# Weight products by three 256-column matmuls in place of one of 512 and one of 256

## The chip, the cores and the metric

The kernel runs on one core of a Trainium2 chip. The metric is the device time of one execution in microseconds, as the median of several runs.

## What is computed

A two-layer decoder trunk with a batch of 1, 256 tokens, and a width of 2048, all in float32. Each layer has a token-mixing half and an MLP half, both with an RMS norm ahead and behind. Cut to what matters:

```python
h = rms_norm(x, norm_mix_pre[i])
z = h @ w_comb                                # 2048 x 6400: 16 RWKV-7 heads and 8 attention heads
y_r, v_r = rwkv7_mix(token_shift(z[..., :N_SHIFT], shift_mu[i]), ...)
y_a = moba_attention(q, k, v)                 # of z[..., N_SHIFT:N_IN]
y = jnp.concatenate([y_r, y_a], axis=-1) @ w_out[i]
x = x + rms_norm(y, norm_mix_post[i])
h = rms_norm(x, norm_mlp_pre[i])
m = jnp.square(jax.nn.relu(h @ w_up[i])) @ w_down[i]     # 2048 -> 8192 -> 2048
x = x + rms_norm(m, norm_mlp_post[i])
```

## The kernel before

Activations lie transposed: 128 features on the partitions, 256 tokens along a row. A product with a weight matrix is made of **weight tiles** of 128 x 128. To keep precision with the fast format fp32r, weights and activations are each split in two parts, high and low. A product is high x high, plus high weights x low activations, plus low weights x high activations.

**Weights.** SyncE fetches 128 x 1024 values at a time, eight weight tiles, into one of four slots `raw[r]` (function `fetch`). ScalarE (ACT) rounds the slot to its high part `whi[r]` (`hi`, L886), and VectorE (DVE) subtracts to get the low part `wlo[r]` (`lo`, L1131). In the mixer GpSimd (POOL) takes two of every twelve low parts (L442). The split runs three slots ahead of TensorE (PE). A slot is free again when `slot_used` counts it.

**Activations.** `hT` and `mT` hold for each 128 features the high and the low part side by side, 2 x 256 columns. So one 512-column matmul with the high weight gives high x high in columns 0 to 255 of a PSUM bank, and high x low in columns 256 to 511. A second matmul of 256 columns adds low weights x high activations to columns 0 to 255. Both are in `tick`, L537 and L538, and for the last of 16 steps the order is turned round, L538 and L540. The profile shows one LDWEIGHTS (PEld) for each MATMUL, 16347 of either.

```python
if not last:
    mm(bank[b0 + b][:, :], whi[r][:, cols], pair, start=first, stop=False)
m = mm(bank[b0 + b][:, 0:SEQ], wlo[r][:, cols], act[:, kt, 0, :], start=False, stop=False)
if last:
    m = mm(bank[b0 + b][:, :], whi[r][:, cols], pair, start=False, stop=True)
```

**Groups.** A `group` is 16 such steps over the input features for two output tiles of 128 features, in two PSUM banks. Four banks let two groups alternate. When a group ends, its result is taken out in two steps: ACT copies the right halves of the two banks to `xl` (`halves`, L894), which counts `half_out`, and DVE adds the left halves (`sums`, L1137), which counts `tile_out`. PE waits for `tile_out` before it writes a bank again.

**Stages of a layer.** First the small projections of 256 (layer 1 also 32) columns ("lora"); then the pairs; then the output projection; then the MLP in four quarters, each of eight up groups and eight down groups. In the up groups DVE adds the halves (L1496), squares the positive part (L1499), ACT writes the high part (L1094) and DVE the low part (L1503). In the down groups DVE adds the halves (L1514), and then adds the sum to `yo` (L1519). Between the stages the norms run: squares on ACT (L920), column sums on PE (L583, L586), and the scaling on DVE.

**Pairs.** The eight pairs of a layer (two RWKV heads of 64 and one attention head of 128 each) go through `mixer`, a long chain of small steps over PE, ACT, DVE and POOL. PE fills the gaps of the chain with steps of three groups of the input projection (`fill`, `pair_ticks`): 7 steps after the first small matmuls (L622 to L624), then it waits for `t1` of DVE (L633), 4 more, then it waits for `btl` (L643), and so on. The order of each engine is written out by hand. `finish(-1)`, at the head of the mixer on ACT and DVE, takes out the group that ended last; `finish(0)` and `finish(1)` take out the other two further down. On DVE, `finish(-1)` stands ahead of the clamp of the key norm (L1202), its reciprocal (L1204), the decay (L1207), the scan (L1209) and `t1` (L1218). On ACT it stands ahead of the tanh of the decay (L952), which DVE's L1207 waits for.

## Time and profile before

| | |
|---|---|
| median of 3 runs | 2931.75 us (2930.35 to 2931.97) |
| span of the profiled execution, first to last instruction | 2927.5 us |
| PE busy, matmuls | 2826.8 us (97%), 16347 instructions |
| PE busy, weight loads | 2377.9 us (81%), 16347 instructions |
| DVE busy | 1805.9 us (62%) |
| ACT busy | 1282.0 us (44%) |
| POOL busy | 327.2 us (11%) |
| TensorE clock | mean 0.989 of full speed |

No time of the profiled execution is given apart from its span, which is 4.2 us below the median; that remainder lies outside the first and the last instruction. Busy time of PE runs from an instruction's start to its modelled end, and matmuls overlap: the distance from one start to the next tells what a matmul costs in a stream, and it is shorter than the mean duration shown. In a timeline a row with x2 is two instructions in a row of one group, shown with the start of the first and their common duration. A wait is shown as the idle time before an instruction and the one that released it.

### The profile page before, as it was taken

The page shows a single profiled execution, that of the slowest core. Times are in us where ns is not written, and L with a number is a line of the kernel's source. Part 1 is how long each engine was busy: PE and PEld are TensorE (multiplying, and loading weights), DVE is VectorE, ACT ScalarE, POOL GpSimd, SP SyncE. Part 2 cuts the span into 40 slices and gives each one's busy share as a digit, 9 for nine tenths or more (in the row PEclk, how much of TensorE's full clock was granted, in tenths as well). Part 3 has the DMA queues.
Part 4 walks back from the last instruction along what each step waited for, and adds up shares of the span by engine and source line. Part 5 has one row for each costly group of instructions (what it writes and reads, how often), then busy time and mean ns, then how long its engine had stood idle before and what let it go on. Part 6 is the DMA issues. An engine that isn't in the chain of part 4 may idle for free.

```text
span 2927.5 us, 50952 instructions
## 1 busy us (share of the span) xinstructions
PE 2826.8 (97%) x16347; PEld 2377.9 (81%) x16347; DVE 1805.9 (62%) x3008; ACT 1282.0 (44%) x2144; POOL 327.2 (11%) x448
## 2 busy tenths in 40 slices
PE   7999999998999999999989999999989999999997
PEld 6777778886888888888767788887868888888886
DVE  6666666656655656556676666666576556565655
ACT  5434333444544444444453343344444444444443
POOL 3111111102000000000132222221020000000002
PEclk9999999999999999999999999999999999999998
DMA  6333333333656555555533333332436565555653
GB/s 183 97 88 92 101 92 88 96 121 110 193 186 186 184 187 180 192 181 186 155 108 98 88 90 93 93 90 87 139 113 192 184 187 183 187 184 187 186 182 112
DMA packets 518313, 415.91 MB, mean 142 GB/s; under 512 B 19422, under 2 KB 515696, under 8 KB 518256
## 3 DMA queue, kind: packets, MB, share of 16 engines
q1 hardware_dynamic: 515888, 412.88, 45.5%
q0 software_dynamic: 2368, 2.32, 0.3%
q8 instruction: 30, 0.49, 0.1%
q14 instruction: 27, 0.22, 0.0%
HBM read 413.03 MB, written 2.10 MB: 142 GB/s over the span
## 4 chain that ended last, share of the span: by engine, by line
PE 89%; DVE 8%; issue 1%; ACT 1%; POOL 0%; DMA 0%; DVEq 0%; ACTq 0%; POOLq 0%; SPq 0%
PE gemm_bank L537 45%; PE gemm_bank L538 24%; PE gemm_bank L540 3%; PE mix_bank L697 2%; PE mix_bank L686 2%; PE mix_bank L695 2%; PE mix_bank L658 1%; DVE b_yo L1172 1%; DVE b_rn L1204 1%; PE mix_bank L659 1%; PE mix_bank L715 1%; PE mix_bank L719 1%; DVE b_yo L1155 1%; PE mix_bank L729 1%; PE mix_bank L725 1%
## 5 line engine op out<-in xcount | busy, mean ns | idle before, releaser
L537 PE MATMUL gemm_bank<-b_hT,b_whi 128*128 128x512 f32 x3420 | 1273.2, 411 | 28.1 <-DVE b_hT L1152 14.4
L1131 DVE TENSOR_TENSOR b_wlo<-b_raw,b_whi 128x1024 fp32r<-128x1024 f32 x745 | 908.0, 1232 | 498.0 <-ACT b_whi L886 496.7
L886 ACT ACTIVATE b_whi<-b_raw 128x1024 fp32r<-128x1024 f32 x777 | 806.3, 1055 | 489.4 <-PE gemm_bank L538 484.1
L538 PE MATMUL gemm_bank<-b_hT,b_wlo 128*128 128x256 f32 x3648 | 1016.8, 283 | 0.0
L537 PE MATMUL gemm_bank<-b_mT,b_whi 128*128 128x512 f32 x2400 | 856.7, 400 | 1.7 <-DVE b_yo L1137 1.7
L537 PEld LDWEIGHTS gemm_bank<-b_hT,b_whi 128*128 128x128 f32 x3420 | 647.0, 189 | 201.4 <-issue 51.7
L538 PE MATMUL gemm_bank<-b_mT,b_wlo 128*128 128x256 f32 x2560 | 706.8, 281 | 0.0
L538 PEld LDWEIGHTS gemm_bank<-b_hT,b_wlo 128*128 128x128 f32 x3648 | 693.7, 190 | 14.2 <-issue 5.3
L537 PEld LDWEIGHTS gemm_bank<-b_mT,b_whi 128*128 128x128 f32 x2400 | 451.0, 188 | 110.6 <-issue 4.3
L538 PEld LDWEIGHTS gemm_bank<-b_mT,b_wlo 128*128 128x128 f32 x2560 | 483.8, 189 | 7.1
L894 ACT ACTIVATE b_xl<-gemm_bank 128x256 f32<-128x256 f32 x389 | 127.8, 381 | 302.2 <-PE gemm_bank L540 296.8
L478 POOL TENSOR_TENSOR b_gs<-b_gs,b_zt 128x256 f32<-128x256 f32 x56 | 38.1, 681 | 1498.4 <-ACT b_zt L920 1495.2
L996 ACT ACTIVATE b_U<-mix_bank 64x128 f32<-64x128 f32 x64 | 17.3, 271 | 239.9 <-PE mix_bank L715 239.9
L978 ACT ACTIVATE b_yo<-mix_bank 128x128 f32<-128x128 f32 x160 | 44.6, 279 | 165.9 <-PE mix_bank L686 165.9
L697 PE MATMUL mix_bank<-b_yo 128*128 128x64 f32 x640 | 115.0, 273 | 0.0
L1275 DVE COPY_PREDICATED b_yo<-b_lvl,mix_bank 128x128 f32<-128x128 uint8 x128 | 42.6, 333 | 104.3 <-PE mix_bank L697 104.3
L442 POOL TENSOR_TENSOR b_wlo<-b_raw,b_whi 128x1024 fp32r<-128x1024 f32 x32 | 76.1, 2378 | 188.7 <-DVE b_wlo L1131 172.4
L695 PE MATMUL mix_bank<-b_yo 128*128 128x64 f32 x512 | 95.3, 267 | 0.0
L697 PEld LDWEIGHTS mix_bank<-b_yo 128*128 128x128 f32 x640 | 93.4, 192 | 0.7
L435 POOL TENSOR_TENSOR b_yo<-b_zt 128x256 f32<-128x256 f32 x32 | 20.9, 670 | 645.0 <-DVE b_zt L1137 645.0
L1514 DVE TENSOR_TENSOR b_xl<-gemm_bank,b_xl 128x256 f32<-128x256 f32 x128 | 48.4, 420 | 71.6 <-ACT b_xl L894 71.6
L1496 DVE TENSOR_TENSOR b_AR<-gemm_bank,b_xl 128x256 f32<-128x256 f32 x128 | 48.5, 421 | 65.2 <-ACT b_xl L894 65.2
(229 smaller groups left out, 2627.8 us busy)
## 6 DMA issues: line engine op xcount, KB each, us to landing
b_raw<-in_w_up SPq DMA_DIRECT2D x256, 512.0 KB
b_raw<-in_w_down SPq DMA_DIRECT2D x256, 512.0 KB
b_raw<-in_w_in SPq DMA_DIRECT2D x384, 256.0 KB
b_raw<-in_w_out SPq DMA_DIRECT2D x48, 512.0 KB
b_raw<-in_w_out SPq DMA_DIRECT2D x32, 256.0 KB
b_raw<-in_w_in SPq DMA_DIRECT2D x8, 512.0 KB
b_yo<-in_x SPq DMA_DIRECT2D x2, 1024.0 KB, 6.9
out<-b_raw SPq DMA_DIRECT2D x8, 256.0 KB, 2.5
```

Of the source, the lines that this page charges most:

```text
L442: nc.gpsimd.tensor_tensor(wlo[at][:, :], raw[at][:, :, :].rearrange("p a b -> p (a b)"), whi[at][:, :].bitcast(F32), ALU.subtract).then_in ...
L537: mm(bank[b0 + b][:, :], whi[r][:, cols], pair, start=first, stop=False)
L538: m = mm(bank[b0 + b][:, 0:SEQ], wlo[r][:, cols], act[:, kt, 0, :], start=False, stop=False)
L540: m = mm(bank[b0 + b][:, :], whi[r][:, cols], pair, start=False, stop=True)
L686: m = mm(packed(mb[2 + w][:, at:at + HEAD], lv), G[:, unit, 2, :], blocks(TT[:, unit, 0, :], lv, 0), start=True, stop=True)
L695: mm(packed(mb[w][:, at:at + HEAD], lv), TT[:, unit, 1, :], blocks(X[:, unit, :], lv, 0), start=True, stop=True)
L697: m = mm(packed(mb[w][:, P + at:P + at + HEAD], lv), X[:, unit, :], blocks(TT[:, unit, 1, :], lv, 1), start=True, stop=True)
L886: f(whi[r][:, :], raw[r][:, :, :].rearrange("p a b -> p (a b)"), ACT.Copy).then_inc(hi_done, 1)
L894: f(xl[:, b, :], bank[b0 + b][:, SEQ:2 * SEQ], ACT.Copy).then_inc(half_out, 1)
L1131: tt(wlo[r][:, :], flat(raw[r][:, :, :]), whi[r][:, :].bitcast(F32), ALU.subtract).then_inc(lo_done, 1)
L1496: tt(hid(b), bank[2 * g + b][:, 0:SEQ], xl[:, b, :], ALU.add).then_inc(up_sum, 1)
L1514: tt(xl[:, b, :], bank[2 * g + b][:, 0:SEQ], xl[:, b, :], ALU.add).then_inc(down_sum, 1)
```

## The change

In `tick` the high weight is used by two matmuls of 256 columns, with the high and with the low activations, and the low weight by one, and all three add into columns 0 to 255 of the bank. The order is the same for all 16 steps. The bank then holds the finished sum, and the halves need no adding. The same is done for the 32-column projection of layer 1.

- ACT copies each finished tile from PSUM straight to its place in `zt` or `yo` (`tiles_to`) and counts `tile_out`; `sums` is gone from DVE. As ACT now writes the places that DVE wrote, it waits ahead of it for their last readers (`free`).
- Up groups: ACT takes relu from PSUM to `AR`, then its square as the high part, while DVE squares into `xl` and subtracts.
- Down groups: ACT does nothing for the bank; DVE waits for the slot and adds the bank to `yo` at once.
- ACT's wait for `used_y` in `y_squares` is made a separate one (`wait_alone`).

```diff
@@ tick, PE
-                pair = act[:, kt, :, :].rearrange("p a b -> p (a b)")
                 for b in range(2):
                     cols = slice(256 * j + P * b, 256 * j + P * b + P)
-                    if not last:
-                        mm(bank[b0 + b][:, :], whi[r][:, cols], pair, start=first, stop=False)
-                    m = mm(bank[b0 + b][:, 0:SEQ], wlo[r][:, cols], act[:, kt, 0, :], start=False, stop=False)
-                    if last:
-                        m = mm(bank[b0 + b][:, :], whi[r][:, cols], pair, start=False, stop=True)
+                    into = bank[b0 + b][:, 0:SEQ]
+                    mm(into, whi[r][:, cols], act[:, kt, 0, :], start=first, stop=False)
+                    mm(into, whi[r][:, cols], act[:, kt, 1, :], start=False, stop=False)
+                    m = mm(into, wlo[r][:, cols], act[:, kt, 0, :], start=False, stop=last)
@@ ACT
-            def halves(k, d, tiles, b0, n=2):
+            def tiles_to(dest, k, d, b0, n=2):
                 act.wait_ge(slot_used, k + 4 * d + 1)
-                if not (isinstance(tiles, int) and tiles <= 0):
-                    act.wait_ge(tile_out, tiles)
                 for b in range(n):
-                    f(xl[:, b, :], bank[b0 + b][:, SEQ:2 * SEQ], ACT.Copy).then_inc(half_out, 1)
+                    f(dest(b), bank[b0 + b][:, 0:SEQ], ACT.Copy).then_inc(tile_out, 1)
...
+                def free(g, n):
+                    if g == -1:
+                        act.wait_ge(l_shift, 2 + 3 * l)
+                        act.wait_ge(e["pair_done"], n + 1)
+                    if g == 1:
+                        act.wait_ge(e["shifted"], 3 * n + 2)
...
                     def finish(g):
-                        halves(k + 11 + 4 * g, i * 3, t + 4 + 2 * g + i * 6, (2, 2, 0)[g + 1])
+                        free(g, PAIRS * l + i)
+                        tiles_to(place((1, 2, 0)[g + 1]), k + 11 + 4 * g, i * 3, (2, 2, 0)[g + 1])
...
+                                    f(AR[:, b, :, :].rearrange("p a b -> p (a b)"), bank[2 * g + b][:, 0:SEQ],
+                                      ACT.Relu).then_inc(up_relu, 1)
...
-                                      ACT.Copy).then_inc(up_hi, 1)
+                                      ACT.Square).then_inc(up_hi, 1)
@@ DVE
-            def sums(tiles, b0, dest, n=2):
-                for b in range(n):
-                    dve.wait_ge(half_out, tiles + b + 1)
-                    tt(dest(b), bank[b0 + b][:, 0:SEQ], xl[:, b, :], ALU.add).then_inc(tile_out, 1)
...
-                                    dve.wait_ge(half_out, T + b + 1)
-                                    tt(hid(b), bank[2 * g + b][:, 0:SEQ], xl[:, b, :], ALU.add).then_inc(up_sum, 1)
+                                    dve.wait_ge(up_relu, M + b + 1)
+                                    tt(xl[:, b, :], hid(b), hid(b), ALU.mult).then_inc(up_square, 1)
...
+                                dve.wait_ge(slot_used, k + 36 + 4 * g + qq * 64 + i * 8)
                                 for b in range(2):
-                                    dve.wait_ge(half_out, T + b + 1)
-                                    tt(xl[:, b, :], bank[2 * g + b][:, 0:SEQ], xl[:, b, :],
-                                       ALU.add).then_inc(down_sum, 1)
-                                for b in range(2):
-                                    dve.wait_ge(down_sum, M + b + 1)
                                     at = bass.ds(i * 4 + 2 * g + b, 1)
-                                    tt(yo[:, at, :], yo[:, at, :], xl[:, b, :].unsqueeze(1),
+                                    tt(yo[:, at, :], bank[2 * g + b][:, 0:SEQ].unsqueeze(1), yo[:, at, :],
                                        ALU.add).then_inc(tile_out, 1)
```

**Where instructions move, PE, end of a pair's mixer and start of the next one.** Before (L537 and L540 are the 512-column matmuls, L538 the one of 256; L622 to L624 are the first matmuls of the mixer):

```order
L537 MATMUL gemm_bank<-b_hT,b_whi 128x512
L538 MATMUL gemm_bank<-b_hT,b_wlo 128x256 x2
L540 MATMUL gemm_bank<-b_hT,b_whi 128x512
L538 MATMUL gemm_bank<-b_hT,b_wlo 128x256
L540 MATMUL gemm_bank<-b_hT,b_whi 128x512
L274 REGISTER_ALU
L274 COMPARE_AND_BRANCH
L622 MATMUL mix_bank<-b_lact,b_lw 128x256 [waits l_shift,l_tanh,m_lw_in,l_ready,m_n2_root,m_pair_done]
L623 MATMUL mix_bank<-b_lact,b_lw 128x256
L624 MATMUL mix_bank<-b_lact,b_lw 128x256
L537 MATMUL gemm_bank<-b_hT,b_whi 128x512 [waits lo_done,hi_done,tile_out]
```

With the change (L535 and L536 take the high weight, L537 the low one):

```order
L535 MATMUL gemm_bank<-b_hT,b_whi 128x256
L536 MATMUL gemm_bank<-b_hT,b_whi 128x256
L537 MATMUL gemm_bank<-b_hT,b_wlo 128x256
L535 MATMUL gemm_bank<-b_hT,b_whi 128x256
L536 MATMUL gemm_bank<-b_hT,b_whi 128x256
L537 MATMUL gemm_bank<-b_hT,b_wlo 128x256
L273 REGISTER_ALU
L273 COMPARE_AND_BRANCH
L619 MATMUL mix_bank<-b_lact,b_lw 128x256 [waits l_shift,l_tanh,m_lw_in,l_ready,m_n2_root,m_pair_done]
L620 MATMUL mix_bank<-b_lact,b_lw 128x256
L621 MATMUL mix_bank<-b_lact,b_lw 128x256
L535 MATMUL gemm_bank<-b_hT,b_whi 128x256 [waits lo_done,hi_done,tile_out]
```

Each weight tile has three matmuls instead of two; nothing else on PE changes place, and the first product after L621 still waits for `tile_out`.

**DVE at the same place.** Before:

```order
L1379 TENSOR_TENSOR b_mT<-b_yf,b_mT 128x256
L1130 REGISTER_ALU
L1131 TENSOR_TENSOR b_wlo<-b_raw,b_whi 128x1024 [waits hi_done]
L274 REGISTER_ALU
L274 COMPARE_AND_BRANCH
L1137 TENSOR_TENSOR b_zt<-gemm_bank,b_xl 128x256 [waits half_out] x2
L1202 TENSOR_SCALAR b_rn<-b_rn 128x256 [waits m_n2_root]
L1204 RECIPROCAL b_rn<-b_rn 128x256 [waits m_n2_max]
L1207 TENSOR_SCALAR b_ldc<-b_eN 128x4x64 [waits m_w_tanh]
```

With the change:

```order
L1384 TENSOR_TENSOR b_mT<-b_yf,b_mT 128x256
L1145 REGISTER_ALU
L1146 TENSOR_TENSOR b_wlo<-b_raw,b_whi 128x1024 [waits hi_done]
L273 REGISTER_ALU
L273 COMPARE_AND_BRANCH
L1209 TENSOR_SCALAR b_rn<-b_rn 128x256 [waits m_n2_root]
L1211 RECIPROCAL b_rn<-b_rn 128x256 [waits m_n2_max]
L1214 TENSOR_SCALAR b_ldc<-b_eN 128x4x64 [waits m_w_tanh]
```

The two adds, which wait for ACT's copies, are gone from between the last subtraction and the clamp.

## Rows read from the trace of the kernel before

**Rows 1.** The page, parts 1 and 4: busy time by engine; the chain that ended last

```profile
PE 2826.8 (97%) x16347; PEld 2377.9 (81%) x16347; DVE 1805.9 (62%) x3008; ACT 1282.0 (44%) x2144; POOL 327.2 (11%) x448
...
PE 89%; DVE 8%; issue 1%; ACT 1%; POOL 0%; DMA 0%; DVEq 0%; ACTq 0%; POOLq 0%; SPq 0%
...
PE gemm_bank L537 45%; PE gemm_bank L538 24%; PE gemm_bank L540 3%; PE mix_bank L697 2%; PE mix_bank L686 2%; PE mix_bank L695 2%; PE mix_bank L658 1%; DVE b_yo L1172 1%; DVE b_rn L1204 1%; PE mix_bank L659 1%; PE mix_bank L715 1%; PE mix_bank L719 1%; DVE b_yo L1155 1%; PE mix_bank L729 1%; PE mix_bank L725 1%
```

**Rows 2.** Groups of instructions, shapes apart: low matmul of every weight tile; a load

```profile
L538 PE MATMUL gemm_bank<-b_hT,b_wlo 128*128 128x256 f32 x3648 | 1016.8, 283 | 0.0
...
L538 PE MATMUL gemm_bank<-b_mT,b_wlo 128*128 128x256 f32 x2560 | 706.8, 281 | 0.0
...
L697 PEld LDWEIGHTS mix_bank<-b_yo 128*128 128x128 f32 x640 | 93.4, 192 | 0.7
```

**Rows 3.** Busy time by stretch, in the MLP: window, length, PE, PEld, DVE, ACT, POOL, clock, DMA

```profile
2400.00:2700.00 300.00, 300.00 (x1701) 260.64 (x1701) 176.59 (x240) 136.42 (x186) 0.00 (x0) 1.00 0.59 188
```

**Rows 4.** Timeline of PE, one group's end in the MLP: start us, us, instruction

```profile
1209.68 0.28 PE L538 MATMUL gemm_bank<-b_mT,b_wlo 128*128 128x256 f32 x1
1209.80 0.40 PE L537 MATMUL gemm_bank<-b_mT,b_whi 128*128 128x512 f32 x1
1210.04 0.40 PE L538 MATMUL gemm_bank<-b_mT,b_wlo 128*128 128x256 f32 x2
1210.28 0.40 PE L540 MATMUL gemm_bank<-b_mT,b_whi 128*128 128x512 f32 x1
1210.51 0.28 PE L538 MATMUL gemm_bank<-b_mT,b_wlo 128*128 128x256 f32 x1
1210.63 0.39 PE L540 MATMUL gemm_bank<-b_mT,b_whi 128*128 128x512 f32 x1
1210.86 0.39 PE L537 MATMUL gemm_bank<-b_mT,b_whi 128*128 128x512 f32 x1
1211.09 0.28 PE L538 MATMUL gemm_bank<-b_mT,b_wlo 128*128 128x256 f32 x1
1211.20 0.40 PE L537 MATMUL gemm_bank<-b_mT,b_whi 128*128 128x512 f32 x1
```

**Rows 5.** Timeline of PEld in the mixer: short matmuls with full weight tiles

```profile
319.95 0.86 PEld L697 LDWEIGHTS mix_bank<-b_yo 128*128 128x128 f32 x7
```

**Rows 6.** Timeline of ACT and DVE, start of the fourth pair's mixer, layer 0

```profile
277.94 0.66 ACT L894 ACTIVATE b_xl<-gemm_bank 128x256 f32<-128x256 f32 x2 [1.49 <-PE gemm_bank L540]
...
278.36 0.76 DVE L1137 TENSOR_TENSOR b_zt<-gemm_bank,b_xl 128x256 f32<-128x256 f32 x2 [1.15 <-ACT b_xl L894]
...
278.62 1.28 ACT L952 ACT_TABLE_LOAD   x1
...
279.03 0.78 DVE L1202 TENSOR_SCALAR b_rn<-b_rn 128x256 f32<-128x256 f32 x1
...
279.84 1.75 DVE L1204 RECIPROCAL b_rn<-b_rn 128x256 f32<-128x256 f32 x1
...
279.91 0.47 ACT L952 ACTIVATE b_eN<-mix_bank,b_drv 128x256 f32<-128x256 f32 x1
...
281.51 0.83 DVE L1207 TENSOR_SCALAR b_ldc<-b_eN 128x256 f32<-128x256 f32 x1
...
284.55 1.32 DVE L1218 SCALAR_TENSOR_TENSOR b_t<-b_sh,b_prm,b_kf 128x256 f32<-128x256 f32 x1 [0.15 <-DVE b_kf L1216]
```

**Rows 7.** Waits of PE, longest in total first: us in total, times, longest us

```profile
PE mix_bank L633 <- DVE b_t L1218: 9.9, 9, 1.5
...
PE mix_bank L643 <- DVE b_btl L1245: 7.8, 9, 1.4
```

**Rows 8.** Timeline of ACT and DVE, end of the last down projection

```profile
2901.59 0.66 ACT L894 ACTIVATE b_xl<-gemm_bank 128x256 f32<-128x256 f32 x2 [7.75 <-PE gemm_bank L540]
...
2902.01 0.76 DVE L1514 TENSOR_TENSOR b_xl<-gemm_bank,b_xl 128x256 f32<-128x256 f32 x2 [6.85 <-ACT b_xl L894]
...
2902.68 0.75 DVE L1519 TENSOR_TENSOR b_yo<-b_yo,b_xl 128x256 f32<-128x256 f32 x2
```

More of the change, by code:

```diff
@@ L793, in _ @@
                         cols = slice(VRES * kt, VRES * kt + P)
[L794 to L799 removed]
+                        into = bank[2][:, 0:SEQ]
+                        mm(into, whi[r][:, cols], hT[:, kt, 0, :], start=kt == 0, stop=False)
+                        mm(into, whi[r][:, cols], hT[:, kt, 1, :], start=False, stop=False)
+                        m = mm(into, wlo[r][:, cols], hT[:, kt, 0, :], start=False, stop=kt == KT - 1)
                     m.then_inc(slot_used, 1)
@@ L1039, in _ @@
                 k, t = start[l, "lora"]
-                group(k, 0, t, 2 * (1 - l))
+                splits(k, 0)
+                tiles_to(lambda b: zt[:, 3 + b, 1:], k + 3, 0, 2 * (1 - l))
                 if l:
@@ L1043, in _ @@
                     hi(k + LEAD)
[L1044 removed]
+                    tiles_to(lambda b: zt[:, 5, 1:], k, 0, 2, 1)
                 act.wait_ge(l_shift, 1 + 2 * l)
@@ L1064, in finish @@
                     if g < 1:
-                        halves(k + 95 + 4 * g, 0, t + 46 + 2 * g, 2)
+                        free(g, PAIRS * l + PAIRS - 1)
+                        tiles_to(place(g + 2), k + 95 + 4 * g, 0, 2)
                 mixer(l, PAIRS - 1, PAIRS * l + PAIRS - 1, t + 46,
@@ L1076, in turn @@
                     for g in range(2):
-                        group(k + 8 + 4 * g, i * 2, t + 4 + 2 * g + i * 4, 2 * g)
+                        splits(k + 8 + 4 * g, i * 2)
+                        tiles_to(hidden(i * 4 + 4 + 2 * g), k + 11 + 4 * g, i * 2, 2 * g)
                         y_squares(2 * l, 4 + 2 * g, i, t + 6 + 2 * g + i * 4)
@@ L1191, in key_norms, with mixer @@
                     ALU.mult).then_inc(e["kk_sq"], 1)
-            def mixer(l, i, n, tiles, step, finish, more=True):
+            def mixer(l, i, n, tiles, step, more=True):
                 V = n + 1
@@ L1468, in step @@
                         lo(k + 92 + j + LEAD)
-                mixer(l, PAIRS - 1, PAIRS * l + PAIRS - 1, t + 46, step, finish, False)
+                mixer(l, PAIRS - 1, PAIRS * l + PAIRS - 1, t + 46, step, False)
                 k, t = start[l, "out"]
-                hidden = lambda a: lambda b: yo[:, bass.ds(a + b, 1), :].rearrange("p a b -> p (a b)")
                 for g in range(2):
                     lo(k + 6 + g + LEAD)
-                    sums(t + 2 * g, 2 * g, lambda b: yo[:, 2 * g + b, :])
                 def turn(i):
```

60 lines of the change are left out of this document (20 added, 40 removed).

## The prediction

> **What bounds the kernel now.** First the page. PE is busy 97% of the span, and the chain that ended last runs 89% over PE; the two lines of `tick` alone make 72% of it [rows 1]. So the kernel lasts as long as PE's stream of weight products, and everything else counts only where PE stands still. Then how much of this work there is: the low matmul occurs once per weight tile, 3648 + 2560 = 6208 times [rows 2]. In a stretch of 300 us inside the MLP PE has no gap, at full clock, with 1701 matmuls, which is 850.5 weight tiles, so one tile lasts 300 / 850.5 = 0.3527 us [rows 3]; 6208 of them make 2190 us, three quarters of the span. ACT and DVE are busy for under 60% of that stretch, so their work is covered there.
>
> The timeline shows how a tile's time divides [rows 4]. From start to start a 512-column matmul takes 0.24, 0.23, 0.23 and 0.23 us (mean 0.232), and a 256-column one 0.12 or 0.11 (five of them in 0.59 us, mean 0.118). The starts are printed to 0.01 us, so these means are good to 2 or 3 ns. Half of 0.232 is 0.116: a column costs about the same in either, and there is hardly a price per matmul. The weight load of the next matmul is hidden: with a 256-column matmul over it, the next one starts 0.12 us later, and the row with x2 is two such matmuls in a row, 1210.04 to 1210.28.
>
> **The PE stream, the first term.** The change takes away 6208 matmuls of 512 columns and adds 12416 of 256, into the same columns; it leaves 768 columns per tile, and adds 6208 weight loads. What three 256-column matmuls in a row cost is not in the trace, two in a row are. Lower bound: full 128 x 128 loads under matmuls of only 64 columns follow each other at (0.86 - 0.19) / 6 = 0.112 us (0.19 is one load's own time) [rows 2, 5], so a tile could not go under 3 x 0.112 = 0.336, which is 0.0167 below now, or -104 us over all tiles. Upper bound: the row of two in a row, 0.12 each, 3 x 0.12 = 0.36, which is +0.0073, or +45 us. By columns alone a tile stays at 0.3527. I take 0.118, the mean of the five [rows 4], as nearest to what will run: 0.354 per tile, +0.0013 x 6208 = **+8 us**.
>
> The Trainium skill, "TensorE: Matmul & The Clock Gate", section on the back-to-back issue gap, gives a matmul N / 2.4 GHz plus about 2.5 ns; by that rule one matmul more per tile would cost 2.5 ns x 6208 = 15.5 us, an estimate. Rows 4 show 2 x 0.118 - 0.232 = 4 ns with an error of as much, so they neither confirm nor refute it; the time it gives stands under the rivals.
>
> **The start of each mixer, the second term.** When a group ends, ACT copies two halves (0.66 us), and DVE adds two (0.76 us) before it clamps, takes the reciprocal (1.75) and reaches the decay at 281.51 [rows 6]. The adds could not begin before 278.36, where DVE had stood idle for 1.15 us waiting for ACT's copy. Without them the clamp can start at 278.36 - 1.15 = 277.21, and with its 0.78 and the 1.75 the reciprocal is through by 279.8. Now the decay must wait for ACT's tanh, which ends at 279.91 + 0.47 = 280.38; ACT's own path (two copies, table load 1.28, tanh) is unchanged, as it copied two tiles before too. With the 0.07 us that a step from engine to engine takes here the decay starts at 280.45, **1.06 us earlier**, and with it all that follows up to `t1` (L1218). What is late next is thus ACT's table load and tanh.
>
> PE waits for exactly these products: 9.9 us in 9 places for `t1`, and 7.8 us in 9 places for `btl`, later on the same chain [rows 7], together 17.7 us, or 1.1 us for each of the 16 pairs. PE also gets its first fill after L624 some 0.3 us sooner, since `tile_out` no longer waits for an add; that only makes it arrive earlier at the same wait, so the chain's 1.06 us is the cap: 16 x 1.06 = 17. In a few pairs the wait is shorter than that, and I take **-16 us**. The new waits of `free` on ACT (`pair_done`, `l_shift`) come while ACT is idle for 1.49 us before the copy [rows 6], and PE itself waits for `pair_done` at L622; I cost them at nothing. If that cover were gone, two waits and the copies behind them would eat up to 0.66 us of the 1.06.
>
> **The ends of stages, the third term.** After the last down group ACT copies, DVE adds two halves (0.76) and then adds them to `yo` (0.75), and the squares of the norm wait for that [rows 8]. With the change DVE's second pair of adds starts when ACT's first copy does. From 2901.59 to 2902.68 that is 1.1 us, and there are two such ends. At the ends of the two output projections ACT's copies stay and the adds go: 0.76 us less a little overlap, about 0.7 each. Together 2 x 1.1 + 2 x 0.7 = 3.6. The handovers from the pairs to the output projection (twice) and into layer 1's small projection wait for the same drain, an estimated 0.5 us each, 1.4 in all. **-5 us**.
>
> **Edits without a price.** In the MLP ACT loses the copies of the down groups, and DVE the adds; `wait_alone` in `y_squares` and the different split of relu and square stand on engines with more than 40% idle time [rows 3], and PE needs a finished bank only one group (32 tiles, 11.3 us) later. Weight fetches keep their order and their pace, which PE's use of the slots sets. That cover would fail only if PE became much faster.
>
> **Sum.** 8 - 16 - 5 = -13 us, 0.4% of the span of 2927.5. That span is 4.2 us below the median of the runs, which I keep: 2931.75 - 13 = **2919 us**.
>
> **The rivals.**
> 1. *Each 256-column matmul takes 0.12 us when it follows one of its own size.* For it: the only two in a row do [rows 4]. Against it: the 512 before and after them are not longer than elsewhere, so that the whole is still 0.35 per tile. Price +45 us against the 21 gained: 2931.75 + 45 - 21 = 2956, slower. The point from which it decides: above 0.1187 us per matmul ((0.3527 + 21 / 6208) / 3) the loss outweighs the gain. With 2.5 ns per additional matmul, as by the rule above, it is 15.5 - 21, so 2926, on the border of no change. I give rival 1 a chance of 0.20.
> 2. *The stream stays as it is but the gain in the mixer doesn't come*, because ACT, which now must have its tiles out before `tile_out` and waits for `free`, gives back what DVE saves, and the chain goes on at ACT's pace. For it: after the change the decay hangs on ACT by 0.6 us more than on DVE (280.38 against 279.8). Then 8 - 5 + 0 to 5: 2932 to 2940; with the stream by columns alone it is no change. Chance 0.10.
> 3. *PE's queue cannot feed three pairs of load and matmul per tile.* There are six instructions in 0.353 us, 0.059 each, where four had 0.088. For it: PE would be bound by issue in the whole stream. Against it: the loads of rows 5, with a matmul to each, went at 0.112 / 2 = 0.056 per instruction. What an instruction costs in a long stream no row shows; at 5% over 0.059 a tile would be 0.370, +108 us: 3018. Chance 0.04.
> 4. *The stream gets faster*, towards the bound of the loads, since no matmul waits for the second half of a 512 wide row: half way to 0.336 it would be -52 - 21, so 2859. Chance 0.04. That the high weight is loaded only once for its two matmuls is possible too, and changes nothing, since loads are hidden.
> 5. My forecast, the stream between 0.1165 (half a 512) and 0.1187 us per matmul, and most of the gain: 0.62.
>
> **How the numbers follow.** The lower end: 3 x 0.1165 = 0.3495, -20 us, with the full 21 gives 2891; I take 2893, which leaves out rival 4. The upper end is rival 1's 2956; only rival 3 lies above. A measurement of this kernel can tell some 0.2%, 6 us, from no change. Faster (under 2926): the forecast and rival 4, less a part of the forecast that lies on the border, 0.62. No change: that part and half of rival 2, 0.15. Slower: rivals 1 and 3 and what is left of 2 and 1's neighbourhood, 0.23. If the likeliest case holds, its own range is 2900 to 2930.
>
> **What the profile afterwards should show.** Three starts per weight tile 0.118 us apart, and about 2550 matmuls in a full stretch of 300 us in the MLP, against 1701; fewer than 2500 speaks for rival 1 (0.120) or 3. PE's matmul count up by 6208, loads likewise. At the mixer's start no adds ahead of the clamp, the clamp at once after DVE's last subtraction, the decay waiting for ACT's tanh; PE's waits for `t1` and `btl` down from 17.7 us to a few. After the last down group one pair of DVE adds, and the norm's squares 1.1 us earlier. The prediction would be wrong if the distance of 256-column matmuls is above 0.1187, or if a pair's mixer gets shorter by less than 0.5 us at an unchanged stream.

## The result, and the profile after

| | before | with the change |
|---|---|---|
| median | 2931.12 us (2930.35 to 2931.97, 4 runs) | 2962.05 us (2961.27 to 2962.35, 4 runs) |
| span of the profiled execution | 2927.5 us | 2960.4 us |
| ratio | | 1.0106, 95% interval 1.0091 to 1.0120 |

The change costs 1.1%, 31 us. The forecast of 2919 had the wrong sign, and the time lies above the upper end of the range, 2956.

The page of the changed kernel, parts 1 and 4, for [rows 1]:

```profile
PE 2870.0 (97%) x22571; PEld 2732.7 (92%) x22571; DVE 1686.0 (57%) x2619; ACT 1244.9 (42%) x2016; POOL 324.9 (11%) x448
...
PE 90%; DVE 7%; ACT 2%; issue 1%; DMA 0%; POOL 0%; DVEq 0%; ACTq 0%; POOLq 0%; SPq 0%
```

PE has 22571 - 16347 = 6224 matmuls more: one for each of the 6208 weight tiles, and 16 for the projection of 32 columns. DVE has less work, as was meant. PE is as busy as before by share, of a longer span: the time went into PE's own work.

Busy time by stretch in the MLP (window, length, PE, PEld, DVE, ACT, POOL, clock, DMA), for [rows 3], first 300 us, then the first 250 of them; and the timeline of PE and PEld (start us, us, instruction), for [rows 4]:

```profile
2400.00:2700.00 300.00, 300.00 (x2502) 300.00 (x2501) 158.90 (x186) 128.65 (x165) 0.00 (x0) 1.00 0.59 183
2400.00:2650.00 250.00, 250.00 (x2086) 250.00 (x2085) 133.00 (x158) 108.85 (x143) 0.00 (x0) 1.00 0.60 183
```

```profile
2500.08 0.28 PE L535 MATMUL gemm_bank<-b_mT,b_whi 128*128 128x256 f32 x1
2500.20 0.28 PE L536 MATMUL gemm_bank<-b_mT,b_whi 128*128 128x256 f32 x1
2500.32 0.28 PE L537 MATMUL gemm_bank<-b_mT,b_wlo 128*128 128x256 f32 x1
2500.45 0.28 PE L535 MATMUL gemm_bank<-b_mT,b_whi 128*128 128x256 f32 x1
...
2500.09 0.19 PEld L536 LDWEIGHTS gemm_bank<-b_mT,b_whi 128*128 128x128 f32 x1
2500.21 0.19 PEld L537 LDWEIGHTS gemm_bank<-b_mT,b_wlo 128*128 128x128 f32 x1
```

At the same full clock (1.00 in both stretches) a matmul takes 300 / 2502 = 0.1199 us from start to start, and a tile 0.3597 where it took 0.3527. The prediction had named fewer than 2500 matmuls in this stretch as the sign of rival 1; 2502 lies just over it, but 300 / 0.12 is 2500 itself, so that sign was set too tight. The distance, 0.1199, is the better one. A load takes 0.19 and the next begins 0.12 later, so PEld has no gap any more (before 260.64 us of 300). Each load starts together with the matmul ahead of its own: L536's load starts at 2500.09, as L535's matmul does (2500.08), and L536's matmul at 2500.20.

Where the 32.9 us between the spans are follows from the starts of a few instructions that both programs have. The first matmul of a mixer (L622, now L619) and the column sum behind a stage (L583, now L580), from the two timelines; those around the MLP of layer 0 as rows, before and then after:

```profile
696.46 0.59 PE L583 MATMUL mix_bank<-b_gs,b_cst 128*128 128x256 f32 x2
...
1448.16 0.59 PE L583 MATMUL mix_bank<-b_gs,b_cst 128*128 128x256 f32 x2
```

```profile
702.40 0.59 PE L580 MATMUL mix_bank<-b_gs,b_cst 128*128 128x256 f32 x2
...
1467.70 0.38 PE L580 MATMUL mix_bank<-b_gs,b_cst 128*128 128x256 f32 x1
```

| from, to | before, us | after, us | difference |
|---|---|---|---|
| start, first mixer of layer 0 | 68.63 | 71.23 | +2.6 |
| seven pairs, first to last mixer (to 557.55; 562.26) | 488.92 | 491.03 | +2.1 |
| last mixer and output projection (to 696.46; 702.40) | 138.91 | 140.14 | +1.2 |
| MLP (to 1448.16; 1467.70) | 751.70 | 765.30 | +13.6 |
| to the first mixer of layer 1 (1519.31; 1538.10) | 71.15 | 70.40 | -0.8 |
| seven pairs (to 2009.78; 2029.36) | 490.47 | 491.26 | +0.8 |
| last mixer and output projection (to 2149.72; 2170.41) | 139.94 | 141.05 | +1.1 |
| MLP (to 2901.40; 2935.69) | 751.68 | 765.28 | +13.6 |
| to the end | 26.10 | 24.71 | -1.4 |

The two MLPs, where nothing but the stream counts, hold 27.2 of the 32.9: 4096 tiles by 0.0066. Seven pairs hold 7 x 96 = 672 tiles, which at 0.007 would be 4.7 us; they became 2.1 and 0.8 longer. So 6.5 us of tile time do not show in these 14 pairs, where about 1 us for each had been forecast as a gain besides. Of the +2.6 at the start, 0.7 is a longer wait for the first transfer of `x` (7.2 us before, 7.9 after); the rest was not followed.

The waits of PE (us in total, times, longest), after, and the one row of before that [rows 7] do not have:

```profile
PE mix_bank L630 <- DVE b_t L1225: 10.9, 8, 1.7
...
PE mix_bank L640 <- DVE b_btl L1252: 6.4, 8, 1.3
...
PE mix_bank L583 <- ACT b_zt L915: 3.8, 4, 1.0
```

```profile
PE mix_bank L586 <- ACT b_zt L920: 7.0, 4, 1.9
```

The waits for `t1` and `btl` are still there, 17.3 us where they were 17.7. In both kernels PE waits for `t1` in the pairs of layer 0 and for `btl` in those of layer 1. The waits at the ends of stages fell by 3.2.

The start of the fourth pair's mixer in the changed kernel, for [rows 6], with POOL beside it:

```profile
281.04 0.66 ACT L887 ACTIVATE b_zt<-gemm_bank 128x256 f32<-128x256 f32 x2 [1.58 <-PE gemm_bank L537]
281.74 1.28 ACT L947 ACT_TABLE_LOAD   x1
283.03 0.47 ACT L947 ACTIVATE b_eN<-mix_bank,b_drv 128x256 f32<-128x256 f32 x1
...
278.99 1.22 DVE L1146 TENSOR_TENSOR b_wlo<-b_raw,b_whi 128x1024 fp32r<-128x1024 f32 x1
280.13 0.29 DVE L1209 TENSOR_SCALAR b_rn<-b_rn 128x256 f32<-128x256 f32 x1
280.45 1.75 DVE L1211 RECIPROCAL b_rn<-b_rn 128x256 f32<-128x256 f32 x1
283.54 1.82 DVE L1214 TENSOR_SCALAR b_ldc<-b_eN 128x256 f32<-128x256 f32 x1 [1.33 <-ACT b_eN L947]
...
280.29 4.92 POOL L441 TENSOR_TENSOR b_wlo<-b_raw,b_whi 128x1024 fp32r<-128x1024 f32 x2 [12.87 <-DVE b_wlo L1146]
```

And POOL's row of the kernel before, which the prediction did not use:

```profile
277.29 4.90 POOL L442 TENSOR_TENSOR b_wlo<-b_raw,b_whi 128x1024 fp32r<-128x1024 f32 x2 [12.32 <-DVE b_wlo L1131]
```

The first half went as forecast: the clamp follows at once on the subtraction, the reciprocal is done 1.3 us before the tanh, and the decay starts 0.04 us after it. But the decay now lasts **1.82 us**, where it had lasted 0.83, and ends at 285.36. POOL's two subtractions end at 285.21. In the kernel before the decay ended at 281.51 + 0.83 = 282.34, and POOL at 277.29 + 4.90 = 282.19. In both kernels it ends 0.15 us after POOL, and not only here: the same holds, to 0.01 us, in 14 of the 16 pairs of either trace (in layer 0 the decay lasts 0.83 or 0.84 before and 1.78 to 1.82 after, in layer 1 0.83 or 0.84 and 1.73 or 1.74). Only the first pair of each layer, where POOL's work lies elsewhere, is different. POOL itself starts 0.08 us after DVE's last low part ahead of the mixer, before (277.21, 277.29) and after (280.21, 280.29), and from that start to the end of the decay it is 5.05 us before and 5.07 us after. So the chain did not get shorter.

### The profile page after: what moved, and what is told of

Same layout as the page of the kernel before. It is cut to its first block, busy times and chain, and to the rows that moved or that the text cites. A ratio compares the mean times of both kernels' runs of the same rounds, so it can differ in the third digit from the quotient of the medians.

```text
span 2960.4 us, 62488 instructions
## 1 busy us (share of the span) xinstructions
PE 2870.0 (97%) x22571; PEld 2732.7 (92%) x22571; DVE 1686.0 (57%) x2619; ACT 1244.9 (42%) x2016; POOL 324.9 (11%) x448
## 4 chain that ended last, share of the span: by engine, by line
PE 90%; DVE 7%; ACT 2%; issue 1%; DMA 0%; POOL 0%; DVEq 0%; ACTq 0%; POOLq 0%; SPq 0%
PE gemm_bank L535 25%; PE gemm_bank L536 24%; PE gemm_bank L537 24%; PE mix_bank L694 2%; PE mix_bank L683 2%; PE mix_bank L692 2%; PE mix_bank L655 1%; DVE b_yo L1181 1%; DVE b_yo L1164 1%; PE mix_bank L656 1%; DVE b_ldc L1214 1%; PE mix_bank L712 1%; PE mix_bank L716 1%; PE mix_bank L726 1%; PE mix_bank L722 1%
## 5 line engine op out<-in xcount | busy, mean ns | idle before, releaser
L881 ACT ACTIVATE b_whi<-b_raw 128x1024 fp32r<-128x1024 f32 x777 | 815.6, 1056 | 718.7 <-PE gemm_bank L537 713.9
L535 PE MATMUL gemm_bank<-b_hT,b_whi 128*128 128x256 f32 x3648 | 1081.0, 296 | 23.5 <-DVE b_hT L1161 14.4
L536 PE MATMUL gemm_bank<-b_hT,b_whi 128*128 128x256 f32 x3648 | 1036.6, 284 | 0.0
L537 PE MATMUL gemm_bank<-b_hT,b_wlo 128*128 128x256 f32 x3648 | 1035.9, 284 | 0.0
L535 PEld LDWEIGHTS gemm_bank<-b_hT,b_whi 128*128 128x128 f32 x3648 | 703.2, 193 | 66.3 <-issue 50.8
L535 PE MATMUL gemm_bank<-b_mT,b_whi 128*128 128x256 f32 x2560 | 729.4, 285 | 0.6 <-ACT b_yo L887 0.6
L536 PE MATMUL gemm_bank<-b_mT,b_whi 128*128 128x256 f32 x2560 | 724.8, 283 | 0.0
L537 PE MATMUL gemm_bank<-b_mT,b_wlo 128*128 128x256 f32 x2560 | 724.8, 283 | 0.0
L536 PEld LDWEIGHTS gemm_bank<-b_hT,b_whi 128*128 128x128 f32 x3648 | 703.9, 193 | 0.4
L537 PEld LDWEIGHTS gemm_bank<-b_hT,b_wlo 128*128 128x128 f32 x3648 | 702.6, 193 | 0.0
L535 PEld LDWEIGHTS gemm_bank<-b_mT,b_whi 128*128 128x128 f32 x2560 | 491.4, 192 | 4.2 <-issue 3.0
L536 PEld LDWEIGHTS gemm_bank<-b_mT,b_whi 128*128 128x128 f32 x2560 | 491.5, 192 | 0.0
L537 PEld LDWEIGHTS gemm_bank<-b_mT,b_wlo 128*128 128x128 f32 x2560 | 491.4, 192 | 0.0
L991 ACT ACTIVATE b_U<-mix_bank 64x128 f32<-64x128 f32 x64 | 17.3, 271 | 241.1 <-PE mix_bank L712 241.1
L1104 ACT ACTIVATE b_AR<-gemm_bank 128x256 f32<-128x256 f32 x128 | 42.2, 382 | 124.2 <-PE gemm_bank L537 124.2
```

What stands on the lines that cost most here:

```text
L535: mm(into, whi[r][:, cols], act[:, kt, 0, :], start=first, stop=False)
L536: mm(into, whi[r][:, cols], act[:, kt, 1, :], start=False, stop=False)
L537: m = mm(into, wlo[r][:, cols], act[:, kt, 0, :], start=False, stop=last)
L881: f(whi[r][:, :], raw[r][:, :, :].rearrange("p a b -> p (a b)"), ACT.Copy).then_inc(hi_done, 1)
L1104: f(AR[:, b, :, :].rearrange("p a b -> p (a b)"), bank[2 * g + b][:, 0:SEQ], ACT.Relu).then_inc(up_relu, 1)
```

## Experiments

**Two questions:** is the 0.12 us of a matmul a price of writing the same columns three times, of issuing, or of loading weights; and what holds the mixer.

### The split alone

The kernel before, with the 512-column matmul cut in two that write the two halves of the bank; all else, the adds too, stays.

```diff
-                        mm(bank[b0 + b][:, :], whi[r][:, cols], pair, start=first, stop=False)
-                    m = mm(bank[b0 + b][:, 0:SEQ], wlo[r][:, cols], act[:, kt, 0, :], start=False, stop=False)
...
+                    mm(bank[b0 + b][:, 0:SEQ], whi[r][:, cols], act[:, kt, 0, :], start=first, stop=False)
+                    mm(bank[b0 + b][:, SEQ:], whi[r][:, cols], act[:, kt, 1, :], start=False, stop=last,
+                       skip_group_check=True)
+                    m = mm(bank[b0 + b][:, 0:SEQ], wlo[r][:, cols], act[:, kt, 0, :], start=False, stop=last)
```

> The kernel before with its 512-column matmul cut in two of 256 that write the same two halves of the bank; all else, the copies and adds too, as before. Theory 1 (what costs is a 256-column matmul that follows another of its size, 0.120 us instead of the 0.3527/3 = 0.1176 of a column's share): tile 0.360, +0.0073 x 6208 = +45 us, less a little for the mixer: 2970 to 2980. Theory 2 (what costs is that three matmuls in a row add into the same columns): the split leaves two of three in different columns, tile about 0.353, 2931 to 2940.

Measured: 2970.07 us (2968.68 to 2970.76), 1.0131 of before (1.0114 to 1.0148). The same 250 us in the MLP:

```profile
2400.00:2650.00 250.00, 250.00 (x2086) 250.00 (x2085) 147.07 (x203) 113.96 (x159) 0.00 (x0) 1.00 0.58 180
```

2086 matmuls, exactly as with the whole change. Theory 1 had that. The price is that of the third matmul with its load; which columns it writes does not matter. The rest of the change, the adds that go, is worth 2970.07 - 2962.05 = 8.0 us. Of that, 3.2 are the ends of stages. In the mixers it is little: seven pairs take 491.76 and 492.74 us here, and 491.03 and 491.26 with the whole change, 2.2 us less in 14 pairs. And already with the adds in place the pairs grew by only 2.8 and 2.3 us where their tiles should have cost 4.7: part of a longer stream falls into PE's waits. The rest of the 8.0 is not settled: the MLPs of this profile take 765.8 and 767.3 us, those of the changed kernel 765.3 twice, and an MLP that is 1.5 us longer also turns up in kernels whose MLP is unchanged (751.9 and 753.4 us in the kernel before with one low part moved, below).

### Is it the load? Fewer columns, smaller weights

Two kernels from the changed one, and one from the one before. In 14 of the 16 steps of each MLP group, either only 192 of the 256 columns are computed, or only 64 of a tile's 128 output features, so that loads are of 128 x 64. The products that are left out are missing in the result.

```diff
@@ 192 columns
-                    into = bank[b0 + b][:, 0:SEQ]
...
+                    N = 192 if mlp[0] and not first and not last else SEQ
+                    into = bank[b0 + b][:, 0:N]
+                    mm(into, whi[r][:, cols], act[:, kt, 0, 0:N], start=first, stop=False)
...
@@ 64 output features, in the changed kernel
-                    into = bank[b0 + b][:, 0:SEQ]
+                    M = 64 if mlp[0] and not first and not last else P
+                    cols = slice(256 * j + P * b, 256 * j + P * b + M)
+                    into = bank[b0 + b][0:M, 0:SEQ]
```

> The changed kernel with all matmuls of the MLP but those of the first and last step of a group on 192 columns instead of 256 (64 tokens lack most of their MLP sums). Theory 1a (the weight load sets the pace): still about 0.117 to 0.120 us from start to start, about 2960 us in all. Theory 1b (the columns set it, with a price per matmul): 0.090 to 0.093, 3584 tiles x 3 x 0.028 = about 300 us less, 2640 to 2670.

> The changed kernel with weight tiles of 128 x 64 in the MLP but for the first and last step of a group (half of the output features lack most of their sums), 256 columns as before. Theory 1a (the load sets the pace): the load takes half the time, and a matmul goes by its columns, 0.109 to 0.112 us, 3584 x 3 x 0.009 = 97 us less, about 2865. Theory 1b: 0.120 as now, 2960.

> The same cut of the weight tiles in the kernel before. If a load that runs beside the columns slows them down, the 512-column matmul too gets faster than 0.2355 us (towards 0.216), and a tile goes from 0.353 to 0.325 to 0.336: 60 to 100 us less, 2830 to 2870. If the load only matters where it is longer than the columns, the 512 stays at 0.235 and only the 256 may gain 0.005: 2910 to 2931.

The last of this set has 96 of 128 features:

> As weights_64, with tiles of 128 x 96 in the middle steps of the MLP. If a load costs the stream in proportion to its columns over 64, a matmul takes 0.1133 + half of 0.0067 = 0.1167 us, 2926 in all. If the cost comes only with the full 128 (a load nearly as long as its cover): 0.1133, 2893. If it is there in full at 96: 0.120, 2961.

Measured: 2874.75, 2892.53, 2886.43 and 2918.52 us, one run each. The stretch of 250 us in the MLP, first of the kernel before, then of these four in this order:

```profile
2400.00:2650.00 250.00, 250.00 (x1418) 217.20 (x1418) 148.96 (x203) 114.60 (x158) 0.00 (x0) 1.00 0.59 188
```

```profile
2400.00:2650.00 250.00, 250.00 (x2222) 250.00 (x2221) 138.67 (x159) 110.20 (x133) 0.00 (x0) 1.00 0.64 195
```

```profile
2400.00:2650.00 250.00, 250.00 (x2191) 250.00 (x2190) 137.57 (x159) 110.48 (x136) 0.00 (x0) 1.00 0.62 192
```

```profile
2400.00:2650.00 250.00, 250.00 (x1467) 186.03 (x1466) 152.30 (x206) 117.33 (x158) 0.00 (x0) 1.00 0.61 192
```

```profile
2400.00:2650.00 250.00, 250.00 (x2149) 250.00 (x2149) 136.74 (x161) 111.29 (x142) 0.00 (x0) 1.00 0.60 187
```

None of the four came out at a time that had been expected: 192 columns and half loads lie between the two theories, with and without the change, and 96 features (2918.5 us) lie nearest to the 2926 of a cost in proportion. So the stretches are read by themselves. In such a stretch 2 of 16 steps are still whole. Taking these out, at the price they have in the unchanged kernel, gives a tile in the reduced steps:

| matmuls per tile | loads 128 x 64 | 128 x 96 | 128 x 128 | on average per whole load, against a half one |
|---|---|---|---|---|
| two, 512 and 256 columns | 0.339 | | 0.3526 | 13.5 ns / 2 = 6.8 ns |
| three of 256 | 0.340 | 0.3475 | 0.3595 | 19.7 ns / 3 = 6.6 ns |

With half loads two and three matmuls cost the same within 1 ns, so there the third matmul has no price of its own. With whole loads a tile gets dearer by the number of its loads, by 6.6 to 6.8 ns for each on average. In the kernel before it is not spread evenly: read to the nanosecond in the same stretch, the mean distance from the start of a 512-column matmul to the next start is 0.2366 us with whole loads and 0.2276 with half ones, 9.0 ns more; that of a 256-column one is 0.1169 and 0.1125, 4.4 ns more. The load that runs under the 512-column matmul has 0.23 us of room for its 0.19, and the distance is longer all the same. So **a load that fits under its matmul is still not shown to be free**. With 192 columns a matmul takes 0.1115 us instead of the 0.09 of three quarters of 0.12: close to the 0.112 at which whole loads followed each other in [rows 2, 5], a second limit, which these runs meet only below 256 columns.

These kernels halve the width of the matmul together with that of the load. A price of the wide matmul itself would not depend on how many matmuls share 768 columns, and this one does; but since every matmul has its load, a price of each wide matmul would look the same. By what the load slows the stream down, no run shows.

**What holds the mixer.** The decay starts right behind ACT's tanh, and is slow itself. Theory P of the following expectations says that POOL's subtractions keep DVE's short steps waiting, theory A that the length of these steps is their own.

### POOL's work in pieces

POOL's 1024-column subtraction is cut in four of 256, so that DVE's steps get in between. In the second pair of kernels POOL's copies that clear buffers (behind the subtractions) wait for `t1` besides.

```diff
-                    nc.gpsimd.tensor_tensor(wlo[at][:, :], raw[at][:, :, :].rearrange("p a b -> p (a b)"),
-                                            whi[at][:, :].bitcast(F32), ALU.subtract).then_inc(lo_done, 1)
+                    for a in range(0, 1024, 256):
+                        piece = slice(a, a + 256)
+                        part = nc.gpsimd.tensor_tensor(wlo[at][:, piece],
+                                                       raw[at][:, :, :].rearrange("p a b -> p (a b)")[:, piece],
+                                                       whi[at][:, piece].bitcast(F32), ALU.subtract)
+                    part.then_inc(lo_done, 1)
@@ the second pair of kernels
+                wait_alone(pool, e["t1_ready"], n + 1)
```

> The changed kernel with POOL's two low parts per pair (4.9 us, two instructions) cut into eight instructions of 256 columns. Theory P (DVE's decay of 1.83 us stands behind POOL's long instruction and ends when that ends, 285.37 against 285.2, so the chain's pace is POOL's): the decay falls to 0.4 to 1.0 us, the chain comes 0.8 to 1.3 us earlier in all 16 pairs, PE's waits for t1 and btl fall from 17.3 us to a few: 2945 to 2951. Theory A (the decay waits for ACT, and its length is its own): no change, 2962.

> The same cut of POOL's instructions in the kernel before. Theory P: there the clamp (0.78 us against 0.29 in the changed kernel) and the decay (0.83) both stood behind POOL; without that the chain comes 0.9 to 1.1 us earlier, 14 to 17 us in all: 2914 to 2918. Theory A: the clamp waits for the two adds and ACT, the decay for the reciprocal, 2931 or at best 5 us less.

> As after_pieces, and POOL's eight copies that reset TT (2.5 us) wait until DVE has made t1. In layer 0 t1 takes 1.32 us while they run, in layer 1, where they run later, 0.48. Theory P (POOL's copies hold up DVE as well): t1 falls to 0.5 us in layer 0 and the time by up to 0.8 us for each of its 8 pairs, 3 to 6 us below after_pieces. Theory A: t1's length is its own, and the copies come later: no change or slower than after_pieces.

> Both edits in the kernel before. Theory P: 3 to 6 us below before_pieces, about 2911, and faster than both kernels. Theory A: 2931.

| kernel | us | ratio to before |
|---|---|---|
| changed, pieces | 2961.69 (2961.64 to 2963.55) | 1.0106 (1.0089 to 1.0123) |
| before, pieces | 2936.09 (2934.06 to 2938.44) | 1.0015 (1.0005 to 1.0024) |
| changed, pieces and copies later | 2960.30 (2959.72 to 2963.13) | 1.0099 (1.0082 to 1.0116) |
| before, pieces and copies later | 2931.08 (2928.89 to 2931.97) | 0.9996 (0.9987 to 1.0006) |

The first of them at the same place:

```profile
283.12 0.60 DVE L1218 TENSOR_SCALAR b_ldc<-b_eN 128x256 f32<-128x256 f32 x1 [1.33 <-ACT b_eN L951]
283.75 1.12 DVE L1220 TENSOR_TENSOR_SCAN b_cs<-b_cst,b_ldc 128x260 f32<-128x260 f32 x1
284.79 0.76 DVE L1224 TENSOR_SCALAR b_kf<-b_ta,b_drv 128x256 f32<-128x256 f32 x1
285.48 0.83 DVE L1225 TENSOR_SCALAR b_ta<-b_ta 128x256 f32<-128x256 f32 x1
...
279.88 6.28 POOL L443 TENSOR_TENSOR b_wlo<-b_raw,b_whi 128x256 fp32r<-128x256 f32 x8 [12.88 <-DVE b_wlo L1150]
```

Theory P had expected 2945 to 2951 and 2914 to 2918 us for the first two, so as a cure this failed, and the kernel before even got 4 us slower. As for the theory, it gives a hint. The decay falls from 1.82 to 0.60, but eight pieces last 6.28 us where two whole ones had 4.92, and the two steps behind the scan, 0.38 each before, now last 0.76 and 0.83. POOL ends at 286.16, and several steps of DVE now last longer by a little each, where one had been held for long. With the copies put later the kernel before gets back 5.0 us of that, as much as had been expected, but not for the reason given: `t1`, 1.32 us in layer 0 of the kernel before [rows 6], lasts 0.51 with pieces alone and 0.48 with the later copies. What gained the 5.0 us was not followed. The changed kernel hardly moves.

### POOL's work nearly gone

POOL's two low parts of a pair are made for 64 of their 1024 columns only; the other 960 columns keep older values, so that part of the computation is left out.

```diff
-                    nc.gpsimd.tensor_tensor(wlo[at][:, :], raw[at][:, :, :].rearrange("p a b -> p (a b)"),
-                                            whi[at][:, :].bitcast(F32), ALU.subtract).then_inc(lo_done, 1)
+                    nc.gpsimd.tensor_tensor(wlo[at][:, 0:64], raw[at][:, 0, 0:64],
+                                            whi[at][:, 0:64].bitcast(F32), ALU.subtract).then_inc(lo_done, 1)
```

> The changed kernel with POOL's two low parts per pair computed for 64 of 1024 columns only (the rest of these low weights is stale, so the work is left out, not moved). Theory P (DVE's chain ends its decay when POOL's 4.9 us end): the decay takes 0.3 to 0.4 us from ACT's tanh on, 1.4 us earlier per pair, PE's waits at the two lines fall from 17.3 us to under 5, 2962 - 12 to 17 = 2945 to 2950. Theory A (the chain's length is its own): 2962. after_pieces, in which the pieces' own overhead gave back what they freed, leaves this open.

> The same left out of the kernel before. Theory P: the clamp takes 0.3 and not 0.78 us, the reciprocal ends 0.5 us earlier, and the decay ends 0.9 to 1.0 us earlier than in the kernel before: 2931 - 10 to 15 = 2916 to 2921. The gap to after_short_pool then shows what the change costs without POOL in the way: 41 us of stream less the ends of stages (4) and 0.5 us per pair of the chain (8): some 29.

Measured: 2940.91 us (2939.98 to 2942.92), 1.0032 of before (1.0021 to 1.0044), from the changed kernel; 2909.64 (2907.29 to 2910.13), 0.9926 (0.9909 to 0.9942), from the one before. DVE and POOL at the same place, first the changed kernel, then the one before; then the waits of PE in the latter:

```profile
279.97 0.30 DVE L1214 TENSOR_SCALAR b_ldc<-b_eN 128x256 f32<-128x256 f32 x1 [1.34 <-ACT b_eN L947]
280.30 0.70 DVE L1216 TENSOR_TENSOR_SCAN b_cs<-b_cst,b_ldc 128x260 f32<-128x260 f32 x1
...
276.72 0.79 POOL L441 TENSOR_TENSOR b_wlo<-b_raw,b_whi 128x64 fp32r<-128x64 f32 x2 [12.87 <-DVE b_wlo L1146]
```

```profile
274.66 0.28 DVE L1202 TENSOR_SCALAR b_rn<-b_rn 128x256 f32<-128x256 f32 x1
...
276.64 0.31 DVE L1207 TENSOR_SCALAR b_ldc<-b_eN 128x256 f32<-128x256 f32 x1
```

```profile
PE mix_bank L633 <- DVE b_t L1218: 0.6, 1, 0.6
...
PE mix_bank L643 <- DVE b_btl L1245: 0.2, 1, 0.2
```

The decay lasts 0.30 instead of 1.82 (changed) and 0.31 instead of 0.83 (before), the clamp of before 0.28 instead of 0.78. PE's 17 us of waits for this chain are gone, in either kernel, and 21 and 22 us with them, 4 and 6 us more than theory P had expected at most; where these come from was not followed. That POOL's subtractions hold the chain is shown: nothing else was changed, and theory A had expected no change. The distance between the two kernels stays at 2940.91 - 2909.64 = 31 us, of which their MLPs hold 27.0. With no hold on DVE, PE has almost no wait left there for the missing adds to shorten.

### The same with all of the work done

In the changed kernel POOL makes one of its two low parts, and DVE the other, between the reciprocal and the decay, where it had stood idle for 1.33 us. DVE's wait for `lo_done` moves there too.

```diff
-                for j in range(2):
+                for j in range(1):
@@ DVE, behind the reciprocal
+                step(-1)
```

> The changed kernel, correct in full: of the two low parts per pair POOL makes the first only, and DVE makes the second (1.2 us) between the reciprocal and the decay, where it waits 1.33 us for ACT's tanh. Theory P: POOL is done 2.4 us sooner, the decay ends 1.0 to 1.4 us earlier, 2962 - 12 to 17 = 2945 to 2950, which is still above the kernel before. Theory A: the extra 1.2 us on DVE's chain are not free, 2962 or more.

Measured: 2942.53 us (2941.64 to 2943.99), 1.0036 of before (1.0022 to 1.0050), so 19.5 us less than the change.

```profile
278.54 1.50 DVE L1146 TENSOR_TENSOR b_wlo<-b_raw,b_whi 128x1024 fp32r<-128x1024 f32 x1 [0.60 <-POOL b_wlo L441]
279.97 0.38 DVE L1215 TENSOR_SCALAR b_ldc<-b_eN 128x256 f32<-128x256 f32 x1
...
276.03 2.36 POOL L441 TENSOR_TENSOR b_wlo<-b_raw,b_whi 128x1024 fp32r<-128x1024 f32 x1 [12.88 <-DVE b_wlo L1146]
```

DVE makes in 1.50 us what takes POOL 2.36, and the decay takes 0.38. In the kernel before DVE has no such gap. There the clamp was put ahead of the two adds, the first low part was moved to DVE between the clamp and the adds, and POOL keeps the second:

```diff
-                for j in range(2):
+                for j in (1,):
@@ DVE, head of the mixer
-                finish(-1)
-
                 dve.wait_ge(e["n2_root"], V)
                 ts(rn[:, :], rn[:, :], 1e-12, None, ALU.max).then_inc(e["n2_max"], 1)
+                step(-2)
+                finish(-1)
```

> The kernel before with nothing left out: GpSimd makes only the second of its two low parts of a pair, and VectorE makes the first, right behind the clamp, followed by the two adds of the finished group. Theory P (GpSimd's subtractions hold up VectorE's clamp, decay and through them PE): the clamp takes 0.3 us, as nothing of GpSimd runs beside it, GpSimd is through at about 281.2 instead of 282.15, and the decay ends 0.75 to 1.5 us earlier than now; VectorE's own subtraction of 1.2 to 1.5 us eats some 0.4 us of that; so 16 x 0.5 to 0.9 us, 8 to 14 us gained: 2917 to 2923 us, under both kernels. Rival: the longer road to the adds (tile_out later by 1.5 us, PE's first gap longer) gives all of it back: 2930 us or more, with the waits of PE for t1 smaller and the gap behind the first small matmuls of the mixer larger.

Measured: **2915.30 us** (2913.88 to 2915.93), 0.9945 of before (0.9931 to 0.9958): faster than both kernels by 16.5 and 47 us.

```profile
275.60 0.29 DVE L1200 TENSOR_SCALAR b_rn<-b_rn 128x256 f32<-128x256 f32 x1
275.80 1.22 DVE L1131 TENSOR_TENSOR b_wlo<-b_raw,b_whi 128x1024 fp32r<-128x1024 f32 x1
276.93 0.75 DVE L1137 TENSOR_TENSOR b_zt<-gemm_bank,b_xl 128x256 f32<-128x256 f32 x2
277.60 1.74 DVE L1204 RECIPROCAL b_rn<-b_rn 128x256 f32<-128x256 f32 x1
279.26 0.38 DVE L1207 TENSOR_SCALAR b_ldc<-b_eN 128x256 f32<-128x256 f32 x1
...
277.10 2.39 POOL L442 TENSOR_TENSOR b_wlo<-b_raw,b_whi 128x1024 fp32r<-128x1024 f32 x1 [13.68 <-DVE b_wlo L1131]
```

```profile
PE mix_bank L633 <- DVE b_t L1218: 0.9, 5, 0.2
...
PE mix_bank L643 <- DVE b_btl L1245: 0.8, 2, 0.5
```

The clamp takes its 0.29 us, and the subtraction fills the time in which DVE had waited 1.15 us for ACT's copies [rows 6], so that the adds come only 0.12 us later after the mixer's first matmul (0.73 us for 0.61). The decay ends at 279.64, POOL at 279.49. The waits of PE fell from 17.7 to 1.7 us. The seven pairs take 482.51 and 483.82 us against 488.92 and 490.47, 13.1 less in 14 pairs. The decay still ends 0.15 us after POOL, but POOL has one subtraction to make and not two. No run tells what the clamp's new place and the moved subtraction are worth apart.

## Why the prediction was wrong

**The stream: the chosen value.** The step that failed is "I take 0.118, the mean of the five". The right value was the upper bound of the same paragraph, 0.12, from the two 256-column matmuls in a row. Measured are 0.1199, 0.0070 us per tile more than before, 43 us by that stretch (41 by the MLPs alone, 0.0066 x 6208), where +8 had been put down. The five mixed two patterns, with starts printed to 0.01 us. To the nanosecond, over the whole stretch of the kernel before from 2400 to 2650 us, a 256-column matmul between two of 512 takes 0.1169 us, and each of two in a row 0.1200. The argument against rival 1, that the 512-column ones were not longer than elsewhere, compared rows that all carry the cost of a load. The change's own pattern stood in one row, and it should have weighed more than a mean over another pattern. Rival 1 is what came, above its point of decision of 0.1187, and without the 21 us that it counted as gained: 2931.75 + 43, less 3 for the ends and 2 for the mixers, is 2970, and the runs have 2962. Some 4 of these 8 us are stream time that fell into PE's waits (in 14 pairs 9.4 us of tiles, of which 5.1 showed in the split alone), and 2 are the 0.0066 of the MLPs against the 0.0070 of the stretch; the remaining 2 were not followed.

"The weight load of the next matmul is hidden" does not stand either: with its matmul, a whole load costs 6.6 ns or more beside a half one. That the load alone is what costs is argued, not shown, as the matmul was narrowed with it.

The Trainium skill, "TensorE: Matmul & The Clock Gate", section on the back-to-back issue gap, gives the N / 2.4 GHz plus 2.5 ns, on which the prediction drew, for a single matmul by itself; for a stream of pairs of load and matmul it says that both set the spacing. The runs agree with the second: at the same columns the third matmul costs under 1 ns with half loads and 7 ns with whole ones, and neither is 2.5.

**The mixer: the wrong thing came late next.** The step "What is late next is thus ACT's table load and tanh" took DVE's steps at the durations that they had. The decay did start right behind the tanh, as forecast, and then took 1.82 us instead of 0.83. Most of the 0.78 of the clamp and the 0.83 of the decay in [rows 6] was not work but a hold by POOL: with POOL's work nearly gone they take 0.28 to 0.31. The end of the decay was POOL's end plus 0.15 us before and after, and POOL started as soon as DVE's low part was done, so that taking work off DVE behind that point gained nothing. Of -16 us, some 2.2 in 14 pairs came. The result of rival 2 (the gain doesn't come) holds, by another mechanism than it gave; and its first half, that the stream stays as it is, does not.

The Trainium skill, "SBUF — State Buffer", section "SBUF: two separate sides", has the rule that was missed: VectorE and GpSimd share a pair of ports, which one instruction holds for its whole length while the other waits; for VectorE this concerns its two-port modes, or two operands in SBUF. The traces agree: a clamp of 0.28 or 0.29 lasts 0.78 beside a subtraction of POOL, a decay of 0.30 lasts 1.82, until 0.15 us after the end of that subtraction; the reciprocal (1.74 to 1.75 with POOL and without) is not held. In which mode these steps ran, no trace shows.

**The ends of stages: right.** -5 us was the sum, of which 3.6 for the four column sums; PE's wait there fell by 3.2 (7.0 to 3.8). In the last stretch 1.4 us were gained, with 1.1 forecast. The other handovers (1.4 us) were not seen apart.

**Edits without a price: right.** DVE and ACT have 47% and 57% idle time in the stretch of the MLP, and neither holds PE there. ACT's table load and the new waits cost nothing that shows. Rival 3 (PE's queue cannot feed so many instructions) is refuted by the kernel with half loads: it has the same six instructions per tile and takes 0.340 us for them, where rival 3 had 0.370.

## What to carry to other kernels

Before a wide matmul is split, count the weight loads, not only the columns: one more matmul with its whole load made a tile about 7 ns longer at the same number of columns, and 6208 of them cost more than all the adds that they saved. When a short instruction lasts two to six times as long at one place as at another, compare its end with the end of what the other engine does at that moment. If the two go together, the chain ends there, and shortening what stands ahead on its own engine gives nothing. Here one of a pair's twelve subtractions, moved from GpSimd to an idle place of VectorE, with the clamp put ahead of the adds, gained 16.5 us, more than the 13 forecast for the whole change.
